# Earlier weight rounding, sums ahead of the last tile and other PSUM banks at the borders of a seven-product feed-forward

## The reference

```python
x = x + o @ w_out                                   # output projection of the mixer, 1024 x 1024
h = rmsnorm(x, ffn_norm) @ w_gate_up                # 1024 x (2 * 2816)
x = x + (silu(h_a) * h_b) @ w_down                  # 2816 x 1024
# after layer 0 only:
q = rmsnorm(x, b_norm) @ b_wq ; k, v, f = rmsnorm(x, kv_norm) @ w_kvf
```

## Time and profile before

| | us |
|---|---|
| three runs | 1848.87, 1849.56 (median), 1851.31 |
| the profiled execution, its time | 1853.4 |
| its span (first to last instruction) | 1851.6 |
| TensorE busy in the span | 1760.3 (95%) |
| VectorE busy | 1136.0 (61%) |
| ScalarE busy | 889.1 (48%) |
| GpSimd busy | 388.2 (21%) |

### The profile page before, as it was taken

The page is one execution under the profiler, slowest core; times in us unless marked ns, Lnnn a source line. Parts: engine busy times, 40 slices in busy tenths (PEclk is TensorE's granted clock), DMA queues, the critical chain, the costliest instruction groups (busy, mean ns, idle before and its releaser), DMA issues. The chain is left out here.

```text
span 1851.6 us, 42008 instructions
## 1 busy us (share of the span) xinstructions
PE 1760.3 (95%) x16657; PEld 1633.7 (88%) x16657; DVE 1136.0 (61%) x2052; ACT 889.1 (48%) x1613; POOL 388.2 (21%) x306
## 2 busy tenths in 40 slices
PE   7999998879999999989998999999988899999998
PEld 7999997879999999989997677777768899999998
DVE  4757766358693948555553456655554768568481
ACT  5365455446352534445632455555544545435252
POOL 3323322110103030323532011112203020301112
PEclk9999999889999999999999999999999999999999
DMA  5333232222333342333355999999972332323332
GB/s 126 86 102 83 82 98 59 69 74 75 92 90 93 92 114 69 85 110 89 108 166 197 374 386 385 385 374 361 353 281 59 87 107 71 113 69 98 86 98 69
DMA packets 292054, 273.80 MB, mean 148 GB/s; under 512 B 22546, under 2 KB 253043, under 8 KB 291348
## 3 DMA queue, kind: packets, MB, share of 16 engines
q1 hardware_dynamic: 289924, 268.63, 44.6%
q10 hardware_dynamic: 1792, 1.44, 0.3%
q0 software_dynamic: 144, 1.05, 0.2%
HBM read 254.64 MB, written 16.43 MB: 146 GB/s over the span
## 5 line engine op out<-in xcount | busy, mean ns | idle before, releaser
L2118 PE MATMUL ps<-xh,f_l 128*128 128x288 f32 x1056 | 231.7, 299 | 17.6 <-issue 13.8
L2137 PE MATMUL ps<-f_h,f_l 128*128 128x288 f32 x1512 | 206.2, 296 | 0.1
L2137 PEld LDWEIGHTS ps<-f_h,f_l 128*128 128x128 f32 x1512 | 202.8, 189 | 0.4 <-DVE t_small L2463 0.3
L2118 PEld LDWEIGHTS ps<-xh,f_l 128*128 128x128 f32 x1056 | 176.9, 190 | 18.9 <-issue 14.3
L1596 DVE COPY at_kt<-ps 128x512 f32<-128x512 f32 x128 | 88.5, 692 | 129.9 <-PE ps L1290 129.9
L2428 DVE TENSOR_TENSOR xT<-xT,ps 128x576 f32<-128x576 f32 x64 | 48.3, 755 | 178.5 <-PE ps L2137 178.5
L2118 PE MATMUL ps<-xl,f_l 128*128 128x288 f32 x528 | 156.6, 297 | 0.0
L2118 PE MATMUL ps<-f_l 128*128 128x288 f32 x1056 | 156.3, 297 | 0.0
L2118 PEld LDWEIGHTS ps<-f_l 128*128 128x128 f32 x1056 | 146.7, 189 | 0.5
L653 POOL TENSOR_TENSOR a_wl<-a_wraw,a_wh 128x1024 fp32r<-128x1024 f32 x32 | 78.6, 2458 | 201.4 <-ACT a_wh L548 186.2
L408 PE MATMUL ps<-xh,a_wh 128*128 128x288 f32 x512 | 115.2, 304 | 0.1
(11 more groups left out here) (431 smaller groups left out, 4302.5 us busy)
## 6 DMA issues: line engine op xcount, KB each, us to landing
xT<-in_cache_k SPq DMA_DIRECT2D x40, 512.0 KB, 5.9
xT<-in_cache_v SPq DMA_DIRECT2D x40, 512.0 KB, 6.6
a_wraw<-in_a_w_in SPq DMA_DIRECT2D x32, 512.0 KB, 4.2
f_h_plain<-in_cache_k SPq DMA_DIRECT2D x30, 512.0 KB, 6.3
xl_plain<-in_cache_v SPq DMA_DIRECT2D x30, 512.0 KB, 6.3
f_h_plain<-in_cache_v SPq DMA_DIRECT2D x30, 512.0 KB, 6.7
xl_plain<-in_cache_k SPq DMA_DIRECT2D x29, 512.0 KB, 6.3
a_wraw<-in_w_gate_up SPq DMA_DIRECT2D x44, 256.0 KB, 3.9
```

The lines of the kernel that those rows point to most:

```text
L2118: mm = pe.matmul(place(m, pos), wt[:, at], combination(2 * q, part, b), start=pos in (0, 1, 3) and t == 0 and i == 0, stop=t == len(pairs) ...
L2137: mm = pe.matmul(ps[:, first + a, 0:HALF], wt[:, at], hidden(i, part)[:, a * HALF:(a + 1) * HALF], start=opens and t == 0 and y == 0, stop ...
```

## The change

1. ScalarE, "o" units: `round_weights(n + 2)` stands ahead of `stream(n)` instead of behind it.
2. At n = 7: ScalarE does round_part(0), (1), (2) ahead of stream(7) and (3), (4) behind it (before: (0) behind stream(6), the rest behind stream(7)). VectorE does low_part(0), fold S1, fold S2, low_part(1), low_part(2) ahead of add(7).
3. The "d" unit ahead of a "g" unit puts its tile 1 into banks 4 and 5. The wait that guarded banks 2 and 3 in the next "g" unit now looks at the unit before that one.
4. The last four "d" units of layer 0: `finished` is split by tile, so that tile 0 is rounded and squared one step after it is taken (at pos 2, in the first of the four at pos 3); `low` and `accumulate` of the even tiles move up into the same unit, of the odd ones to pos 1 and 2 of the next. After the last unit only tile 7 is left (before: 6 and 7), and `weigh(TAIL + 1)` stands behind one low and one accumulate instead of behind two accumulates, and ahead of one low and one accumulate.

```diff
     def out_banks(n, tile):
+        if tile == 1 and kind(n + 1) == "g":
+            return 4
         return DOWN_BANKS[tile][(n - KD) % 2]
...
-                    if kind(n - 1) == "d" and pos == (0 if m % 2 else 1):
-                        pe.wait_ge(e["taken"], last_take(m - 1) + 1)
+                    if kind(n - 2) == "d" and pos == (0 if m % 2 else 1):
+                        pe.wait_ge(e["taken"], last_take(m - 2) + 1)
...
-                def finished(n):
-
-                    j = UNITS[n][2]
-                    for a in range(2):
-                        act.wait_ge(e["taken"], take[n - KD, closing(n, a)] + 1)
-                        act.activation(k.xh[:, 2 * j + a, :], k.xT[:, 2 * j + a, :], ACT.Copy).then_inc(e["xhigh"], 1)
-                    for a in range(2):
-                        square(KD + 2 * j + a)
+                def finished(n, tile):
+
+                    f = 2 * UNITS[n][2] + tile
+                    act.wait_ge(e["taken"], take[n - KD, closing(n, tile)] + 1)
+                    act.activation(k.xh[:, f, :], k.xT[:, f, :], ACT.Copy).then_inc(e["xhigh"], 1)
+                    square(KD + f)
...
                     if kind(n) == "o":
-                        stream(n)
                         if n + 2 < KD:
                             round_weights(n + 2)
-                        if n == KD - 2:
-                            round_part(0)
                         if n == KD - 1:
-                            for s in range(1, AHEAD):
+                            for s in range(3):
+                                round_part(s)
+                        stream(n)
+                        if n == KD - 1:
+                            for s in range(3, AHEAD):
                                 round_part(s)
...
+                            if heads and n >= TAIL - ROWS and pos == (3 if own(n) else 2):
+                                finished(n, 0)
                             if heads and n >= TAIL - ROWS and pos == 3:
-                                finished(n)
+                                finished(n, 1)
...
                         if n == KD - 1:
                             low_part(0)
+                            fold(KD, S1)
+                            fold(KD, S2)
+                            low_part(1)
+                            low_part(2)
                         add(n)
                         cross(n)
...
                         if n == KD - 1:
-                            fold(KD, S1)
-                            fold(KD, S2)
-                            low_part(1)
-                            low_part(2)
                             fold(KD, S3)
...
-                            if last and pos in (1, 2):
-                                low(2 * UNITS[n][2] - 3 + pos)
+                            if last and pos == 1:
+                                low(2 * UNITS[n][2] - 1)
+                            if last and pos == 2:
+                                accumulate(KD + 2 * UNITS[n][2] - 1)
                             low_part(base[n - KD] + pos + LEAD)
...
-                            if last and pos == 3:
-                                for f in (2 * UNITS[n][2] - 2, 2 * UNITS[n][2] - 1):
-                                    if f > 0:
-                                        accumulate(KD + f)
+                            if heads and n >= TAIL - ROWS and pos == 3:
+                                low(2 * UNITS[n][2])
+                                if UNITS[n][2] > 0:
+                                    accumulate(KD + 2 * UNITS[n][2])
                             if n == TAIL - 1 and pos in (1, 3):
                                 weigh(TAIL + (pos - 1) // 2)
...
                         if heads and n == TAIL - 1:
-                            for f in (KD - 2, KD - 1):
-                                low(f)
-                            for f in (KD - 2, KD - 1):
-                                accumulate(KD + f)
+                            low(KD - 1)
+                            accumulate(KD + KD - 1)
```

## The result

The changed kernel took 1818.01 us (median of 4 runs, 1815.51 to 1821.20) against 1849.7 before (4 runs, 1848.87 to 1851.31): ratio 0.9829, 95% interval 0.981 to 0.9848, so 31.7 us less. The profiled execution took 1819.67 us with a span of 1817.8. In the new kernel most lines of `trunk` stand two or three further down (2385 is 2388, 2344 is 2347, 2393 and 2395 are 2396 and 2398, 2415 is 2418, 2428 is 2431).

The account below looks back on a forecast made before the run. TensorE, busy 95% of the span, bounds the kernel, so only its idle time and the low clock behind it can be won: 22.1 - 1.8 + 5.6 + 5.6 = 31.5 us, from 1849.56 to 1818.1 us, range 1812 to 1826.

Parts of the forecast that it names:

- Part 1: Output projections: rounding weights first removes TensorE's stall for GpSimd's low parts, 22.1 us won; lower bound 14.7.
- The condition: Output projections: VectorE's two chains take 12.8 us per pair, what two units take, so TensorE sees no delay.
- Part 2: Border into the feed-forward: sums moved ahead of tile 7 don't pay, 0.9 us lost per layer, 1.8 in all.
- U + 11.05: Border: unit 8's third product (pos 2) starts 11.05 us after unit 7's end (U), before 11.57.
- its price at 1.4 us on one product: Border: the low clock, which before fell on pos 1 (3.0 us for 1.6), now costs pos 2 1.4 us.
- Part 3: "g" units behind "d" units: all six waits for the residual to leave PSUM go, 5.6 us won, bounds 4 and 6.
- Part 4: End of layer 0's trunk: mean(1) comes sooner, 3.8 us idle time plus 1.8 low clock, 5.6 won.
- the first: Rival, projection and border: GpSimd doesn't hold VectorE up, tile 6 on time, +1.3 us per layer, 1813.7 us; chance 0.15.
- the second: Rival, projections: GpSimd's hold on VectorE makes every unit take 8.2 us; slower, 1853.7 us; chance 0.05.
- the third: Rival, trunk's end: GpSimd goes ahead of the last accumulate, 0.9 us won instead of 5.6, 1822.8 us; chance 0.14.
- the fourth: Rival, projections: weights' loads or another wait replace the stall; half the gain lost 1829 us, all 1840; chance 0.06.
- five rows of idle time: TensorE's waits that the change touches: 7.4 + 7.3, 13.8, 5.6 and 4.7 us, together given as 38.7 us.

Follow-up runs that it names:

- first trace without part 2: Changed kernel with the border's old order of sums and block rounding restored, other changes kept, first run: 1813.51 us.
- the interleaved one: Changed kernel with the first product's snapshot ahead of stream(7) and the sums laid into gaps of tile 7's chain: 1811.81 us, ratio 0.9784.
- the changed kernel's second trace: Changed kernel repeated unaltered, on the same chip as a repeat with the border's old order: 1818.47 us, ratio 0.9822.
- filling the wait: Changed kernel with 40 matmuls on unused data between pos 1 and pos 2 of each layer's first gate unit: 1813.54 us, ratio 0.9795.
- the test of the lock: Changed kernel with the first subtraction of cross reading one operand from PSUM instead of SBUF (values wrong): 1817.65 us.
- part 1 alone: Kernel before with only round_weights(n + 2) moved ahead of stream(n): 1828.41 us, ratio 0.9876.
- part 4 undone: Changed kernel with finished, low and accumulate of the last four "d" units as before, tiles 6 and 7 finished together: 1823.30 us, ratio 0.9851.
- earlier snapshot: Changed kernel with the first product's snapshot ahead of stream(7) on ScalarE, waiting for accumulate(6) instead of accumulate(7): 1813.64 us, ratio 0.9787.
- second run without part 2: Changed kernel with the border's old order, run once more on the same chip as a repeat of the changed kernel: 1815.48 us, ratio 0.9809.
- part 3 undone: Changed kernel with tile 1 of "d" units always in banks 2 and 3 and the old wait: 1823.90 us, ratio 0.9855.

## Why the prediction was right

The median came at 1818.0, forecast 1818.1. The mechanisms held, but a hit to 0.1 us is luck: the steps were off by up to 1.6 us each, and these errors happened to cancel against the profile's place above its median (last point).

- *Part 1* was forecast at 22.1 and measured at 22.2 alone, 23.1 in the stages. The condition, that VectorE keeps up though GpSimd holds it, was the risk of the forecast, and it went as worked out: tile 6 about 2.0 us late (1.8 forecast), no wait of TensorE. The excess of 1.1 is all in layer 0, where 0.8 of it is that the matmuls of units 2 to 7 ran some 2% faster than elsewhere (6.26 us per unit in the mean). The first trace without part 2 and the interleaved one show it too, the other ten traces have 6.40; the changed kernel's second trace is among those ten, so no edit explains it, and it is left open.
- *Part 2* was forecast as a loss of 0.9 per layer. Against the one trace of before, the border was longer by 1.4 and 0.9 us in the changed kernel's first trace and by 0.6 and 0.8 in its second. The loss is shown in layer 1, where no trace with part 2 reaches one without; in layer 0 it is within the spread. Pos 2 was forecast at U + 11.05 and came at U + 10.94 or 10.95 in every border of the changed kernel's two traces but one; that one, at 11.28, is the border behind the faster units. Mis-sized was the clock: I put its price at 1.4 us on one product in both kernels. Before, it also slowed pos 2 by 0.5 (2.09 us for 1.6), which I left out, and behind the new wait it was low for longer still (a mean of 0.54 over 5.57 us is 5.1 us at the lower level, the 0.53 over 4.40 us of rows 2 is 4.1); filling the wait won 1.5 to 2.4.
- *Part 3*: 5.6 forecast, 7.2 measured. I took the idle time shown as the price; the start behind a gap costs more.
- *Part 4*: 5.6 forecast, 5.3 in the stages and 5.3 between the medians: 3.9 of idle time (3.8 forecast) and 1.4 of low clock, for which I had put 1.8. The last accumulate went ahead of GpSimd's subtraction by 0.6 us (786.40 against 786.99), for which I had reckoned 0.5.
- The rivals: the first (VectorE not held) is refuted by the trace and by the test of the lock; the second (the lock paces the projection) by units of 6.40 us; the third and the fourth by the mean and by part 1 alone.
- Outside the change the two profiled executions differ by -1.33 and +0.71 us, which nothing in it explains. The stages saved more than forecast (+1.6 in part 3, +1.0 in part 1, against -0.6 in part 2 and -0.3 in part 4), 33.8 us in all, while the medians differ by 31.7, since the old profile lay 3.8 above its median and the new one 1.7. That these two nearly cancel is chance.
- Two small slips of the prediction: its five rows of idle time add up to 38.8, not 38.7, and the first rival is worth 4.4 us (1818.1 to 1813.7), not 4.3. Neither enters the sum.

## What to carry to other kernels

Where an engine waits for a weight preparation that stands behind unrelated work in another engine's queue, put the preparation first and then price the stall with the clock that it costs, not with its idle time alone: here 14.7 us of idle time were worth 22. Before sums are moved ahead of a step, look for what ends last behind that step: here it was a snapshot at the end of the chain, so the sums only pushed the chain back, while the snapshot's own wait was stricter than the buffer needed, and loosening it was worth more than the move. Where a wait can't be taken away, work without use in it can pay by keeping the clock: here 40 matmuls in a wait of 5.3 us.

## What the runs showed of the hardware

- A VectorE instruction with two SBUF inputs that starts during a GpSimd instruction that reads SBUF stands still until that one is done: the subtraction of 128x288 (0.46 us by itself) ended 0.31 to 0.33 us behind GpSimd, whenever in its 2.4 us it had started. With one input from PSUM it ran at its usual 0.45 us beside it. The other way round GpSimd stands still: with part 4 undone, a subtraction that came 0.1 us behind a VectorE multiplication of 1.22 us took 3.38 us in place of 2.37.
- After an idle time of 5.3 us TensorE's granted clock was at its lower level for about 5.1 us, after one of 6.9 us for about 4.1 (both worked out above). A wait of 2.08 us was followed by it too (interleaved border, clock 0.50), one of 1.90 us was not (earlier snapshot, layer 1, clock 1.00).
- How long it stays low differs with all waits the same: behind the wait of 6.50 us in the second run without part 2, pos 3 started at U + 14.61 in layer 0 and at U + 13.34 in layer 1. The changed kernel's first four runs were ordered by their mean granted clock, from 1815.51 us at 0.988 to 1821.20 at 0.984. With the wait filled the clock was 0.990 to 0.993, though the runs still spread over 4.2 us.
- A matmul behind a gap of 0.9 to 1.0 us cost 0.1 to 0.2 us more than the gap (part 3 undone).
